# Seven products for three more units of the first block, column units set later, first weights in one run

## The chip, the core and the metric

The kernel runs on one core of a Trainium2 chip, in f32 throughout. The time is that of one launch, in device microseconds. Five engines run beside each other: TensorE (PE in the rows; its weight loads are PEld), VectorE (DVE), ScalarE (ACT), GpSimd (POOL) and SyncE (SP), which here only starts transfers. Matrix products land in eight banks of PSUM, called G[0] to G[3] and A[0] to A[3].

## The reference, cut to what matters

A sequence of 256 tokens of width 1024 goes through two blocks of two layers each. The first block, per layer:

```
h = rms_norm(x, pre_norm_g[l])
u = h @ w_in[l]                    # 352 + 768 + 768 + 512 + 1024 columns
u_mla, u_sb, u_moba, u_conv, u_gate = split(u)
o_a = mla_attention(...)           # low rank queries and keys, rotary part
o_b = stick_breaking_attention(qb, kb, vb)
o_c = moba_attention(qc, kc, vc, rel_bias)     # the third branch, 4 heads of 64
o_d = conformer_conv(u_conv, ...)  # 31 taps, layer norm, silu, product
y = concat([o_a, o_b, o_c, o_d]) * silu(u_gate)    # four gates of 256 columns
x = x + rms_norm(y @ w_out[l], post_norm_g[l])
```

With 256 tokens the third branch sees one block, so it is causal attention with a bias by distance. The second block is a gated linear attention layer and an attention layer, each followed by a network of width 4096 with a squared relu. Its shifts, scales and gates come from one row c through `w_ada`: `silu(c) @ w_ada[i] + b_ada[i]`.

## The kernel before

**Units.** All large weights come in units of 128 partitions x 2048 values (1 MB) through a ring of six slots, `raw`. SyncE loads unit n once unit n - 6 is released, strictly in order (L481 to L483). A layer of the first block has 30 units: 18 of weights, "w", and 12 column units, "a". A column unit holds columns of `w_ada`; VectorE multiplies it by the row silu(c) and sums along the row, in two halves (L983, `column_half`), for the second block. Two things set their place: the string `ORDER`, which is the order in the ring, and the calls `ada_unit(l, a)` in VectorE's program. I call them a0 to a11.

**The first block on TensorE.** In program order per layer: transposes of the normed tokens; the first weights (two units, `U_MLA0` and `U_MLA1`, each loaded in the first round as four runs of 352 values per partition); the convolution's two units; queries and keys of the second branch; the first branch's low rank products; the values (`U_V0`, `U_V1`); then `unit_t` for the third branch's queries and keys, `U_CQ` into G[0] and `U_CK` into G[1]; transposes of the first branch's queries and keys (L2182); suffix sums of the second branch (L2188 to L2192), which wait for `nl_ready`; and the loop over the four gates. Each turn g of that loop does the gate's unit in G[1] (L2005), the values of the pair before, two turns of transposed probabilities (L2032), and the scores of the next pair. Turn 0 also transposes the convolution's result (L2262), turn 2 transposes its normed form (L2269), which waits for `cnat_ready` of VectorE. A gate's unit waits for `silu_ready`, VectorE's product of the gate before out of G[1] (L1262). `unit_t` is 16 products of 128 x 128 by 256 columns, 32 records in the trace, since an f32 product is two records.

**VectorE in the same place.** Norms, rotary parts, the 31 taps of the convolution (L1030), the second branch's logarithms (L1237 to L1244, sums L1250), masks and row maxima of the scores (L1052, L1055), reciprocals (L1062), gates (L1262), the layer norm of the convolution (L1311 to L1321), and column units a0 to a10 between them. ScalarE does exponentials, tanh of gates, and copies out of PSUM.

**Seven products.** In the second block large products already run in Winograd's form: a 2 x 2 block product by seven products and sums, not eight products. `mixer_weights` (L1759 to L1764) builds four sums of a unit's blocks, `mixer_sums` (L1772 to L1782) adds up the seven results, `token_sums` (L1591 to L1595) builds the sums of the tokens.

**The network of the second block.** 15 groups of seven products; per group g VectorE does half sums, weight sums, rest sums, hidden sums, sums of a later unit, and from group 1 on a column unit of the second layer (`side_unit`). When the last one is done it computes two sets of coefficients (L1071 to L1085). Behind the last group come `seven_sums` (L1667 to L1684), the residual, and the boundary to the next stage.

## Time and profile before

| | |
|---|---|
| median of 3 runs | 970.14 us (969.9 to 970.84) |
| the profiled execution | 970.39 us, span 968.6 us |
| TensorE busy | 955.1 us, 99% of the span |
| VectorE busy | 759.3 us, 78% |
| ScalarE busy | 230.5 us, 24% |
| GpSimd busy | 83.2 us, 9% |
| transfers | 205.39 MB, 212 GB/s |
| granted clock of TensorE | 0.998 |

Times in the rows are microseconds from the start of the span. The first block's layer 0 lies between 7 and 156 us, its layer 1 between 156 and 301 us; from the second branch's values on they run alike, some 146.5 us apart. A busy share tells how full an engine is, not whether it is waited for: that is in the list of waits and in the idle time written in brackets behind a row of the timeline, with what ended it.

### The profile page before, as it was taken

The numbers are of one execution on the slowest core, as the hardware profiler recorded it, in microseconds if no ns is written. First come the engines' busy times: TensorE is split into PE (matmuls) and PEld (weight loads), VectorE is DVE, ScalarE is ACT, GpSimd is POOL, SyncE is SP. The second block draws the span as 40 slices with busy tenths as digits, with TensorE's granted clock in tenths as the row PEclk, the third lists the DMA queues.
The fourth block names the chain that finished last, engine by engine and source line by source line (L and its number), as shares of the span: only waits on it lengthen the run. The fifth ranks groups of instructions, "written<-read, shape, count | busy, mean of one in ns | idle before, by whom it ended". The sixth has DMA issues, their size and how long they took to land. (4 is left out here: it accounts for less than half of the span.)

```text
span 968.6 us, 14456 instructions
## 1 busy us (share of the span) xinstructions
PE 955.1 (99%) x5386; PEld 712.5 (74%) x5386; DVE 759.3 (78%) x1721; ACT 230.5 (24%) x580; POOL 83.2 (9%) x100
## 2 busy tenths in 40 slices
PE   8999999999999999999999999999999999999996
PEld 5858856858867998757777777689994777777764
DVE  2797687697688898999899988955667877766687
ACT  4134434125433222111000000123333200000002
POOL 2100000100001000000001000056830000000000
PEclk9999999999999999999999999999999999999999
DMA  9955553955555756473579677535443255544411
GB/s 347 365 211 210 213 222 133 369 198 231 193 225 208 294 218 256 177 300 132 218 294 357 259 306 261 196 131 196 153 175 137 100 199 174 217 174 174 174 44 44
DMA packets 31213, 205.39 MB, mean 212 GB/s; under 512 B 3655, under 2 KB 4860, under 8 KB 7852
## 3 DMA queue, kind: packets, MB, share of 16 engines
q1 hardware_dynamic: 27884, 190.94, 52.4%
q0 software_dynamic: 3264, 13.57, 3.7%
q8 instruction: 43, 0.70, 0.3%
q14 instruction: 22, 0.18, 0.1%
HBM read 203.42 MB, written 1.07 MB: 211 GB/s over the span
## 5 line engine op out<-in xcount | busy, mean ns | idle before, releaser
L2005 PE MATMUL bank<-hT,raw 128*128 128x256 f32 x704 | 155.6, 381 | 0.0
L2005 PEld LDWEIGHTS bank<-hT,raw 128*128 128x128 f32 x704 | 133.0, 190 | 19.8 <-issue 2.4
L983 DVE CUSTOM_DVE_ANT_0 raw<-raw,crow 128x1024 f32<-128x1024 f32 x96 | 114.1, 1232 | 9.2 <-DMA raw<-units_dram 7.7
L2364 PE MATMUL bank<-yT,arena 128*128 128x512 f32 x224 | 100.8, 593 | 0.5 <-DVE yT L1658 0.5
L2364 PE MATMUL bank<-raw,arena 128*128 128x512 f32 x180 | 86.9, 593 | 0.0
L2364 PEld LDWEIGHTS bank<-yT,arena 128*128 128x128 f32 x224 | 42.4, 190 | 53.3 <-issue 50.6
L2392 PEld LDWEIGHTS bank<-hT,raw 128*128 128x128 f32 x416 | 50.4, 192 | 11.5 <-issue 11.5
L841 ACT ACTIVATE arena<-bank 128x512 f32<-128x512 f32 x26 | 15.5, 598 | 177.6 <-PE bank L2392 177.6
L2392 PE MATMUL bank<-hT,raw 128*128 128x128 f32 x416 | 50.7, 275 | 0.0
L1030 DVE SCALAR_TENSOR_TENSOR arena<-arena 128x256 f32<-128x256 f32 x120 | 49.2, 486 | 0.1
L2364 PEld LDWEIGHTS bank<-raw,arena 128*128 128x128 f32 x180 | 30.1, 191 | 17.2 <-issue 17.2
L2392 PE MATMUL bank<-arena 128*128 128x128 f32 x336 | 42.2, 276 | 0.0
L2392 PE MATMUL bank<-arena,gateT 128*128 128x128 f32 x336 | 42.1, 275 | 0.0
L2392 PEld LDWEIGHTS bank<-arena 128*128 128x128 f32 x336 | 39.8, 192 | 1.2 <-issue 1.2
L2392 PEld LDWEIGHTS bank<-arena,gateT 128*128 128x128 f32 x336 | 39.8, 192 | 0.0
L2085 PE MATMUL bank<-arena 128*128 128x512 f32 x88 | 39.8, 592 | 0.0
L2392 PEld LDWEIGHTS bank<-arena,raw 128*128 128x128 f32 x224 | 29.4, 192 | 13.4 <-issue 13.4
L843 ACT ACTIVATE arena<-bank 128x384 f32<-128x384 f32 x28 | 13.7, 491 | 105.1 <-PE bank L2392 105.1
L2335 PE MATMUL bank<-hT,raw 128*128 128x128 f32 x244 | 37.4, 283 | 0.9 <-ACT hT L700 0.7
L1621 DVE TENSOR_TENSOR arena<-arena 128x256 f32<-128x256 f32 x26 | 11.0, 424 | 32.4 <-ACT arena L841 31.8
L2335 PEld LDWEIGHTS bank<-hT,raw 128*128 128x128 f32 x244 | 33.0, 191 | 3.8 <-issue 2.1
L2085 PEld LDWEIGHTS bank<-arena 128*128 128x128 f32 x88 | 16.6, 190 | 19.7 <-issue 19.6
(473 smaller groups left out, 1782.4 us busy)
## 6 DMA issues: line engine op xcount, KB each, us to landing
raw<-units_dram SPq DMA_DIRECT2D x178, 1024.0 KB, 4.9
arena<-ln_rows_dram POOLq DMA_DIRECT2D x4, 1024.0 KB, 5.9
arena<-gate_scratch POOLq DMA_DIRECT2D x4, 512.0 KB, 6.9
arena<-att_line_dram POOLq DMA_DIRECT2D x4, 512.0 KB, 5.2
arena<-small_dram POOLq DMA_DIRECT2D x2, 896.0 KB, 10.5
raw<-units_dram SPq DMA_DIRECT2D x2, 704.0 KB, 8.0
xt<-x_dram SPq DMA_DIRECT2D x2, 512.0 KB, 5.6
arena<-post_g_dram POOLq DMA_DIRECT2D x2, 512.0 KB, 8.5
```

The costliest lines, as they stand in the source:

```text
L841: act.activation(prod[:, 0:4].rearrange("p i n -> p (i n)"), A[0][:], ACT.Copy).then_inc(prod_ready.sem, 1)
L843: act.activation(prod[:, 4:7].rearrange("p i n -> p (i n)"), A[0][:, 0:3 * P], ACT.Copy).then_inc(prod_ready.sem, 1)
L983: ins = dve.tensor_tensor_reduce(out=w, in0=w, in1=crow[:], scale=1.0, scalar=0.0, op0=ALU.mult, op1=ALU.add, accum_out=dst[:, c:c + 1])
L1030: ins = dve.scalar_tensor_tensor(cacc[:, c, :], xg[:, c, j:j + S], w, cacc[:, c, :], ALU.mult, ALU.add)
L1621: ch.do(dve.tensor_tensor(csum[:, 0:5:4], p[:, 0:1].to_broadcast([P, 2, P]), p[:, 1:3], ALU.add))
L2005: mm = pe.matmul(b[:, c * S:(c + 1) * S], raw[:, s, k * 256 + c * P:k * 256 + (c + 1) * P], act_t[:, k, :], start=(k == 0), stop=(k == KC ...
L2085: mm = pe.matmul(OUT_BANKS[l][j][:], x[c] if isinstance(x, list) else x[:, c], y[c] if isinstance(y, list) else y[:, 512 * c:512 * (c + 1) ...
L2335: mm = pe.matmul(b[:, c * S + t * P:c * S + (t + 1) * P], raw[:, n % SLOTS, k * 256 + c * P:k * 256 + (c + 1) * P], hT[:, k, t * P:(t + 1) ...
L2364: mm = pe.matmul(SB[i][:], x, y, start=g == 0, stop=stop)
L2392: mm = pe.matmul(b[:, i * P:(i + 1) * P], x(k), y(k), start=k == 0, stop=k == 3)
```

## The change

1. Third branch's queries, its keys and the second gate go through seven products: 28 products of 128 x 128 by 128 columns a unit. New on VectorE are `first_tokens` (four additions a layer), `first_weights` (four additions and waits a unit) and `first_outputs` (six). ScalarE copies a unit's seven products out of PSUM in two parts. The keys go to A[2] and G[1], the second gate to G[1] and A[0]. Its tanh is taken from a buffer `early`, and the third gate's unit waits for ScalarE's copy of G[1] in place of VectorE's gate.
2. Column units: a3 (before in the middle of the taps) behind the logarithms; a4 and a5 (before behind the taps and the logarithms) behind the row maxima of the second pair of heads; a6 and a7 behind those of the third pair; a8 behind the normed convolution; a9 as before. `ORDER` is changed to match. In the first network column units go by halves, and from group 8 on they stand half a unit later.
3. The first two units are laid out without gaps, 1408 values in one run per partition.
4. Some small transfers share a semaphore; that is left out here.

```diff
-ORDER = "wwwawwawwawawawa" "wawawawa" "wwawwa"
+ORDER = "wwwawwawwa" "wwwa" "wwaaa" "waa" "wa" "wwawwa"
...
+U_SEVEN = (U_CQ, U_CK, U_G1)
...
-                w = [t.rearrange("p (k n) -> p k n", k=4)[:, :, 0:MLA_IN if s <= U_MLA1 else 512] for t in (raw[:, s, :], units[s, :, :])]
-                sp.dma_start(w[0], w[1]).then_inc(landed[s], 16)
+                c = slice(0, 4 * MLA_IN if s <= U_MLA1 else UNIT)
+                sp.dma_start(raw[:, s, c], units[s, :, c]).then_inc(landed[s], 16)
...
-                wait_used(act, T1 * l, U_CQ)
-                act.activation(qkC[:, 0], G[0][:], ACT.Copy, scale=HD_SCALE).then_inc(qk_ready.sem, 1)
-                wait_used(act, T1 * l, U_CK)
-                act.activation(qkC[:, 1], G[1][:], ACT.Copy).then_inc(qk_ready.sem, 1)
+                act.wait_ge(rope_ready.sem, rope_ready.at(l, 2))
+                for i, (u, b) in enumerate(((U_CQ, G[0]), (U_CK, A[2]))):
+                    scale = (HD_SCALE, 1.0)[i]
+                    act.wait_ge(fhalf_ready.sem, fhalf_ready.at(l, i + 1))
+                    act.activation(first_prod[i][:, 0:4].rearrange("p i n -> p (i n)"), b[:], ACT.Copy,
+                                   scale=scale).then_inc(fprod_ready.sem, 1)
...
+                def gate_copies(g):
+
+                    p = first_prod[(g + 1) % 2]
+                    act.wait_ge(qk_ready.sem, qk_ready.at(l, 2 + g))
+                    act.wait_ge(fhalf_ready.sem, fhalf_ready.at(l, g + 2))
+                    act.activation(p[:, 4:7].rearrange("p i n -> p (i n)"), A[0][:, 0:3 * P], ACT.Copy).then_inc(fprod_ready.sem, 1)
+                    wait_used(act, T1 * l, U_GATE[g])
+                    act.activation(p[:, 0:4].rearrange("p i n -> p (i n)"), G[1][:], ACT.Copy).then_inc(fprod_ready.sem, 1)
+
                 def gate_tanhs(g):
-                    wait_used(act, T1 * l, U_GATE[g])
+                    if g != 1:
+                        wait_used(act, T1 * l, U_GATE[g])
                     if g >= 1:
                         act.wait_ge(silu_ready.sem, silu_ready.at(l, g))
-                    act.activation(th[:].rearrange("p c s -> p (c s)"), G[1][:], ACT.Tanh, scale=0.5).then_inc(gate_tanh.sem, 1)
+                    if g == 1:
+                        act.wait_ge(qk_ready.sem, qk_ready.at(l, 5))
+                    act.activation(th[:].rearrange("p c s -> p (c s)"), gate_in if g == 1 else G[1][:], ACT.Tanh,
+                                   scale=0.5).then_inc(gate_tanh.sem, 1)
...
+            def first_tokens(l):
+
+                dve.wait_ge(ht_act.sem, ht_act.at(l, 12))
+                dve.wait_ge(ht_dve.sem, ht_dve.at(l, 4))
+                b = [[hT[:, 4 * k:4 * k + 4, t * P:(t + 1) * P] for t in range(NT)] for k in range(2)]
+                ch.do(dve.tensor_tensor(first_tsum[:, 0], b[0][1], b[0][0], ALU.subtract))
+                ch.do(dve.tensor_tensor(first_tsum[:, 2], b[1][1], b[0][1], ALU.subtract))
+                ch.sync(1)
+                ch.do(dve.tensor_tensor(first_tsum[:, 1], b[1][1], first_tsum[:, 0], ALU.subtract))
+                ch.sync()
+                dve.tensor_tensor(first_tsum[:, 3], b[1][0], first_tsum[:, 1], ALU.subtract).then_inc(fsum_ready.sem, 1)
+
+            def first_weights(l, i):
+
+                wait_landed(dve, T1 * l, U_SEVEN[i])
+                ch.pass_waits()
+                a, d = first_blocks(U_SEVEN[i]), first_sums[i]
+                ch.do(dve.tensor_tensor(d[1], a[0][0], a[1][0], ALU.subtract))
+                ch.sync()
+                ch.do(dve.tensor_tensor(a[1][0], a[1][0], a[1][1], ALU.add))
+                ch.sync()
+                ch.do(dve.tensor_tensor(d[0], a[1][0], a[0][0], ALU.subtract))
+                ch.sync()
+                dve.tensor_tensor(d[2], a[0][1], d[0], ALU.subtract).then_inc(fsum_ready.sem, 1)
+
+            def first_outputs(l, i, o):
+
+                p, c = first_prod[i % 2], first_tmp
+                dve.wait_ge(fprod_ready.sem, fprod_ready.at(l, 2 * i + 2))
+                ch.pass_waits()
+                ch.do(dve.tensor_tensor(c[:, 0], p[:, 0], p[:, 2], ALU.add))
+                ch.do(dve.tensor_tensor(o[:, 0], p[:, 0], p[:, 1], ALU.add))
+                ch.sync(1)
+                ch.do(dve.tensor_tensor(c[:, 1], c[:, 0], p[:, 3], ALU.add))
+                ch.do(dve.tensor_tensor(c[:, 2], c[:, 0], p[:, 5], ALU.add))
+                ch.sync(1)
+                ch.do(dve.tensor_tensor(o[:, 2:4], c[:, 1:2].to_broadcast([P, 2, P]), p[:, 4:6], ALU.add))
+                ch.sync(1)
+                ch.do(dve.tensor_tensor(o[:, 1], c[:, 2], p[:, 6], ALU.add))
+                ch.sync()
+                dve.sem_inc(qk_ready.sem, 1)
...
+                first_tokens(l)
...
-                taps(0, 12)
-                ada_unit(l, 3)
-                taps(12, 20)
+                taps(0, 20)
...
+                first_weights(l, 0)
+                first_weights(l, 1)
                 taps(20, TAPS)
-                ada_unit(l, 4)
...
-                ada_unit(l, 5)
-                ada_unit(l, 6)
+                ada_unit(l, 3)
+                for i in range(2):
+                    first_outputs(l, i, qkC[:, i].rearrange("p c (t n) -> p (c t) n", t=NT))
...
+                first_weights(l, 2)
                 for j in range(2 * H):
                     if j % 2 == 0:
-                        gate(j // 2)
+                        if j == 2:
+                            first_outputs(l, 2, early)
+                        else:
+                            gate(j // 2)
...
+                        if j == 2:
+                            gate(1)
                         if j < 6:
-                            ada_unit(l, 7 + j // 2)
+                            for a in ((4, 5), (6, 7), (9,))[j // 2]:
+                                ada_unit(l, a)
...
+                        ada_unit(l, 8)
...
-            def side_unit(lay, g, half=range(2)):
-
-                if lay == 0 and AG + g < len(ADA_1):
-                    ada_unit_1(ADA_1[AG + g], AG + g, half)
-                    if AG + g == len(ADA_1) - 1:
+            def side_half(lay, h):
+
+                n = AG + h // 2
+                if lay == 0 and n < len(ADA_1):
+                    ada_unit_1(ADA_1[n], n, (h % 2,))
+                    if n == len(ADA_1) - 1 and h % 2 == 1:
...
-                    if 0 < g < 8:
-                        side_unit(lay, g - 1)
-                    if g in (7, 8):
-                        side_unit(lay, 7, (g - 7,))
-                    if g >= 8:
-                        side_unit(lay, g)
+                    if g > 0:
+                        for h in range(2 * g - 2 + (g > 7), 2 * g + (g > 6)):
+                            side_half(lay, h)
...
+            def first_seven(l, i, b0, b1):
+
+                u = U_SEVEN[i]
+                a, d = first_blocks(u), first_sums[i]
+                h = [[hT[:, 4 * k:4 * k + 4, t * P:(t + 1) * P] for t in range(NT)] for k in range(2)]
+                x = [first_tsum[:, k] for k in range(4)]
+
+                def product(b, c, w, y):
+                    for k in range(4):
+                        mm = pe.matmul(b[:, c * P:(c + 1) * P], w[:, k], y[:, k], start=k == 0, stop=k == 3)
+                    return mm
+
+                def first_bank():
+                    product(b0, 0, a[0][0], h[0][0])
+                    product(b0, 1, a[0][1], h[1][0])
+                    pe.wait_ge(fsum_ready.sem, fsum_ready.at(l, i + 2))
+                    product(b0, 3, d[1], x[2])
+                    return product(b0, 2, d[0], x[1])
+
+                def second_bank():
+                    product(b1, 0, a[1][1], x[3])
+                    pe.wait_ge(fsum_ready.sem, fsum_ready.at(l, i + 2))
+                    product(b1, 2, d[2], h[1][1])
+                    return product(b1, 1, a[1][0], x[0])
+
+                wait_landed(pe, T1 * l, u)
+                pe.wait_ge(fsum_ready.sem, fsum_ready.at(l, 1))
+                if i < 2:
+                    first_bank().then_inc(fhalf_ready.sem, 1)
+                    if i == 1:
+                        pe.wait_ge(fprod_ready.sem, fprod_ready.at(l, 2))
+                    second_bank().then_inc(used[u % SLOTS], 1)
+                else:
+                    second_bank().then_inc(fhalf_ready.sem, 1)
+                    if i > 2:
+                        pe.wait_ge(fprod_ready.sem, fprod_ready.at(l, 2 * i))
+                    first_bank().then_inc(used[u % SLOTS], 1)
...
-                unit_t(T1 * l, U_CQ, hT, G[0])
-                unit_t(T1 * l, U_CK, hT, G[1])
+                first_seven(l, 0, G[0], G[1])
+                pe.wait_ge(upc_ready.sem, upc_ready.at(l, 6))
+                first_seven(l, 1, A[2], G[1])
...
-                    if g >= 1:
+                    if g == 0:
+                        pe.wait_ge(fprod_ready.sem, fprod_ready.at(l, 4))
+                    elif g == 2:
+                        pe.wait_ge(fprod_ready.sem, fprod_ready.at(l, 6))
+                    else:
                         pe.wait_ge(silu_ready.sem, silu_ready.at(l, g))
-                    unit_t(T1 * l, U_GATE[g], hT, G[1])
+                    if g == 1:
+                        pe.wait_ge(pt_ready.sem, 8 * l + 2 * g)
+                        first_seven(l, g + 1, G[1], A[0])
+                    else:
+                        unit_t(T1 * l, U_GATE[g], hT, G[1])
```


TensorE, where layer 0 comes to the third branch's queries and keys; before:

```order
L2015 MATMUL bank<-raw,hT 128x512 x16
L2161 MATMUL bank<-arena 128x256 x4
L2166 MATMUL bank<-arena 128x128 x4
L2005 MATMUL bank<-hT,raw 128x256 x32
L2182 MATMUL bank<-kst,arena 96x128 x16
```


and now:

```order
L2292 MATMUL bank<-arena 128x128 x4
L2173 MATMUL bank<-hT,raw 128x128 x8
L2173 MATMUL bank<-xs,gateT 128x128 x8
L2173 MATMUL bank<-xs,raw 128x128 x4
L2173 MATMUL bank<-hT,gateT 128x128 x4
L2173 MATMUL bank<-xs,raw 128x128 x4
L2173 MATMUL bank<-hT,raw 128x128 x8
L2173 MATMUL bank<-xs,yT 128x128 x8
L2173 MATMUL bank<-xs,raw 128x128 x4
L2173 MATMUL bank<-hT,yT 128x128 x4
L2173 MATMUL bank<-xs,raw 128x128 x4
L2310 MATMUL bank<-kst,arena 96x128 x16
```


The 32 products of 256 columns have become 56 of 128 columns. Those that read only `hT` and `raw` come first in the queries' unit; `gateT` and `yT` hold sums of the weights, `xs` those of the tokens.

VectorE in layer 0, between the row maxima of the second pair of scores and the third gate's product (`L1262`, now `L1344`); `ISA raw,acc<-raw,crow` is half a column unit; before:

```order
L1062 RECIPROCAL rinv<-rsum 128x2 x2
L983 ISA raw,acc<-raw,crow 128x1024
...
L1311 BN_STATS bst<-bank 128x6 x2
L1315 BN_AGGR bag<-bst 128x2 x2
L1317 TENSOR_SCALAR ms<-bag 128x2
L1262 SCALAR_TENSOR_TENSOR gateT<-arena,bank 128x512
...
L1062 RECIPROCAL rinv<-rsum 128x2 x2
L983 ISA raw,acc<-raw,crow 128x1024
...
L1321 TENSOR_SCALAR arena<-bank,bag,rs 128x256 x2
L1262 SCALAR_TENSOR_TENSOR gateT<-arena,bank 128x512
```


and now:

```order
L1143 RECIPROCAL rinv<-rsum 128x2 x2
L1022 ISA raw,acc<-raw,crow 128x1024
...
L1022 ISA raw,acc<-raw,crow 128x1024
...
L1400 BN_STATS bst<-bank 128x6 x2
...
L1106 TENSOR_TENSOR arena<-arena 128x128
...
L1143 RECIPROCAL rinv<-rsum 128x2 x2
L1344 SCALAR_TENSOR_TENSOR gateT<-arena,early 128x512
L1022 ISA raw,acc<-raw,crow 128x1024
...
L1022 ISA raw,acc<-raw,crow 128x1024
...
L1410 TENSOR_SCALAR arena<-bank,bag,rs 128x256 x2
L1022 ISA raw,acc<-raw,crow 128x1024
...
L1344 SCALAR_TENSOR_TENSOR gateT<-arena,bank 128x512
```


Where one column unit stood in front of the convolution's statistics (`BN_STATS`) there are two, the six additions of `first_outputs` (`L1106` and on) follow, the second gate's product stands behind the next maxima, then come two column units in place of one, and one more stands between the normed convolution and the third gate's product.

VectorE at the end of the first network, the last two groups (`gacc` column units, `L1071` to `L1085` the coefficients, `L1667` the first of the seven sums); before:

```order
L1614 TENSOR_TENSOR arena<-raw,arena 128x512
L983 ISA raw,gacc<-raw,crow 128x1024
...
L999 SCALAR_TENSOR_TENSOR gcol<-gacc,colb 128x8
L1071 TENSOR_TENSOR arena<-acc,colb 128x16
...
L1071 TENSOR_TENSOR arena<-acc,colb 128x16
...
L1621 TENSOR_TENSOR arena<-arena 128x2x128
...
L1653 TENSOR_TENSOR yT<-raw 128x512
...
L1658 TENSOR_TENSOR gateT<-gateT,raw 128x512
L1667 COPY arena<-bank 128x512
L1670 TENSOR_TENSOR arena<-arena,bank 128x512
```


and now:

```order
L1704 TENSOR_TENSOR arena<-raw,arena 128x512
L1022 ISA raw,gacc<-raw,crow 128x1024
...
L1711 TENSOR_TENSOR arena<-arena 128x2x128
...
L1743 TENSOR_TENSOR yT<-raw 128x512
...
L1748 TENSOR_TENSOR gateT<-gateT,raw 128x512
L1022 ISA raw,gacc<-raw,crow 128x1024
...
L1038 SCALAR_TENSOR_TENSOR gcol<-gacc,colb 128x8
L1152 TENSOR_TENSOR arena<-acc,colb 128x16
...
L1152 TENSOR_TENSOR arena<-acc,colb 128x16
...
L1757 COPY arena<-bank 128x512
L1760 TENSOR_TENSOR arena<-arena,bank 128x512
```


One half unit and both sets of coefficients have moved from ahead of group 13's rest to behind its last weight sums, directly in front of the seven sums.

## Rows read from the trace of the kernel before

**Rows 1.** The list of TensorE's waits: its line <- what ended the wait: us, times, longest.

```profile
PE bank L2058 <- DMA raw<-units_dram: 0.9, 2, 0.8
...
PE bank L2364 <- DVE yT L1658: 0.5, 1, 0.5
```

**Rows 2.** Busy time of VectorE by stretch: stretch, its length, busy us (instructions), clock, DMA share, GB/s.

```profile
43.48:119.01 75.53, 59.68 (x163) 1.00 0.57 214
191.07:265.48 74.41, 58.85 (x163) 1.00 0.56 212
```

**Rows 3.** VectorE's waits between 191.07 and 265.48 us.

```profile
DVE rinv L1062 <- ACT probs L637: 4.7, 5, 2.4
DVE gateT L1262 <- ACT arena L780: 4.6, 2, 2.9
DVE probs L1052 <- PE bank L2208: 2.6, 1, 2.6
DVE arena L1250 <- PE bank L2190: 2.0, 2, 1.4
```

**Rows 4.** TensorE in order of time: start, us, engine, line, out<-in, xcount [idle before].

```profile
42.83 7.07 PE L2005 MATMUL bank<-hT,raw 128*128 128x256 f32 x32
49.74 0.81 PE L2146 MATMUL bank<-arena 128*128 128x384 f32 x2
...
488.78 1.95 PE L2392 MATMUL bank<-hT,raw 128*128 128x128 f32 x16
...
492.35 1.88 PE L2364 MATMUL bank<-raw,arena 128*128 128x512 f32 x4
```

**Rows 5.** VectorE in order of time, second block's sums.

```profile
331.08 0.29 DVE L1774 TENSOR_TENSOR arena<-arena,bank 128x128 f32<-128x128 f32 x1
...
332.84 0.69 DVE L1759 TENSOR_TENSOR arena<-raw 128x512 f32<-128x512 f32 x1 [0.22 <-DVE arena L1782]
...
334.05 0.68 DVE L1762 TENSOR_TENSOR arena<-arena,raw 128x512 f32<-128x512 f32 x1
334.77 0.69 DVE L1764 TENSOR_TENSOR arena<-raw,arena 128x512 f32<-128x512 f32 x1
```

**Rows 6.** VectorE in order of time, the waits ahead of the column units.

```profile
31.49 0.75 DVE L1015 TENSOR_SCALAR arena<-arena 128x1024 f32<-128x1024 f32 x1 [3.28 <-ACT arena L727]
...
188.78 1.22 DVE L983 CUSTOM_DVE_ANT_0 raw<-raw,crow 128x1024 f32<-128x1024 f32 x1 [5.05 <-DMA raw<-units_dram]
```

**Rows 7.** VectorE's third gate product and TensorE's fourth gate unit, layer 1.

```profile
264.80 0.68 DVE L1262 SCALAR_TENSOR_TENSOR gateT<-arena,bank 128x512 f32<-128x512 f32 x1
...
266.41 7.17 PE L2005 MATMUL bank<-hT,raw 128*128 128x256 f32 x32
```

**Rows 8.** TensorE in order of time, the second unit of first weights.

```profile
12.10 2.63 PE L2058 MATMUL bank<-raw,hT 128*128 128x352 f32 x8 [0.77 <-DMA raw<-units_dram]
```

**Rows 9.** VectorE, then TensorE, at the end of the first network.

```profile
603.04 0.17 DVE L999 SCALAR_TENSOR_TENSOR gcol<-gacc,colb 128x8 f32<-128x8 f32 x1
...
605.14 0.43 DVE L1621 TENSOR_TENSOR arena<-arena 128x256 f32<-128x256 f32 x1 [0.50 <-DVE arena L1085]
...
615.78 0.69 DVE L1672 TENSOR_TENSOR arena<-arena,bank 128x512 f32<-128x512 f32 x1 [0.85 <-PE bank L2364]
616.70 0.69 DVE L1675 TENSOR_TENSOR arena<-arena,bank 128x512 f32<-128x512 f32 x1 [0.24 <-PE bank L2364]
...
619.54 0.69 DVE L1684 TENSOR_TENSOR arena<-arena,bank 128x512 f32<-128x512 f32 x1
...
625.53 0.69 DVE L1391 TENSOR_TENSOR arena<-bank,arena 128x512 f32<-128x512 f32 x1 [0.24 <-PE bank L2434]
...
632.28 1.04 PE L2102 MATMUL bank<-kst,xs 128*128 128x128 f32 x8
```

**Rows 10.** TensorE by stretch behind its last product: length, busy, clock, DMA share, GB/s.

```profile
962.00:964.00 2.00, 0.00 (x0) 1.00 0.53 201
964.00:966.00 2.00, 0.00 (x0) 0.52 0.11 39
```

More of the change, by code:

```diff
@@ L452, in build, with first_blocks @@
         out_block = [gateT[:].rearrange("p a b -> p (a b)")[:, 512 * i:512 * (i + 1)] for i in range(4)]
+        first_tsum = four(flat(xs))
+        first_sums = [[b[:, 512 * i:512 * (i + 1)].rearrange("p (k n) -> p k n", k=4) for i in range(3)]
+                      for b in (flat(gateT), flat(yT), nl, lbeta)]
+        first_sums.append([b.rearrange("p (k n) -> p k n", k=4) for b in (
+            flat(yT)[:, D:D + 512], flat(yT)[:, D + 512:2 * D], flat(cacc))])
+        first_prod = [b[:, 0:7 * P].rearrange("p (i n) -> p i n", i=7) for b in (mu_cn, flat4(qkB))]
+        first_tmp = rt[:].rearrange("p a b c d -> p (a b c d)")[:, 0:3 * P].rearrange("p (i n) -> p i n", i=3)
+        gate_in = early.rearrange("p i n -> p (i n)")
+        def first_blocks(u):
+            w = raw[:, u % SLOTS, :].rearrange("p (k n) -> p k n", k=KC)
+            return [[w[:, 4 * k:4 * k + 4, c * P:(c + 1) * P] for k in range(2)] for c in range(2)]
         def tile_banks(s, t):
@@ L2255, in _ @@
                     turn(8 * l, 2 * g, (A[3], A[0]))
+                    if g == 1:
+                        pe.wait_ge(fprod_ready.sem, fprod_ready.at(l, 2 * g + 3))
                     turn(8 * l, 2 * g + 1, (A[3], A[0]))
@@ L2839, in n_unit @@
 def n_unit(w, c0, half, width=512):
-    u = np.zeros((P, 4, 512), w.dtype)
-    u[:, :, :width] = w[half * 512:(half + 1) * 512, c0:c0 + width].reshape(4, P, width).transpose(1, 0, 2)
-    return u.reshape(P, UNIT)
+    u = np.zeros((P, UNIT), w.dtype)
+    u[:, :4 * width] = w[half * 512:(half + 1) * 512, c0:c0 + width].reshape(4, P, width).transpose(1, 0, 2).reshape(P, 4 * width)
+    return u
 def ada_gate(w, part, a):
```

62 lines of the change are left out of this document (36 added, 26 removed).

## The prediction

> **What bounds the kernel now.** I read the page's busy shares first, which the table above repeats: TensorE is busy 99% of the span. The list of TensorE's waits says what small part of the rest is to be had: two waits on the first weights, 0.9 us, and one on a weight sum of VectorE, 0.5 us [rows 1]. So in the two layers of the first block TensorE never waits, and the reader is to ask of each edit how much room the engine that feeds TensorE has left. That engine is VectorE: I took its busy time between two fixed points of each layer, from the end of column unit a2 (43.48 and 191.07 us) to the end of the third gate's product (119.01 and 265.48 us). It is busy 59.68 of 75.53 us and 58.85 of 74.41 us, so it idles 15.8 and 15.6 us [rows 2]. The list of its waits in layer 1 splits this idle time [rows 3]: 4.7 us on ScalarE's exponentials, 4.6 us on ScalarE's tanh of a gate, 2.6 and 2.0 us on TensorE's scores and suffix sums, and 1.7 us of small waits and gaps.
>
> **What the change gives TensorE.** A unit of 256 columns by plain products is 32 records in 49.74 - 42.83 = 6.91 us. By seven products of 128x128x512 it is 56 records. In the second block 32 such records take 492.35 - 488.78 = 3.57 us, 0.1116 us each [rows 4], so 56 take 6.25 us. Three units a layer and two layers save 6 x 0.66 = 4.0 us of TensorE's work. I cost this saving at nothing for the sum unless VectorE keeps up, which is the next step.
>
> **What it costs VectorE.** Per unit, the weight sums are four 128x512 additions, each waiting for the one before. The second block's sums show a dependent addition 0.72 us behind its predecessor (334.05, 334.77), and the last one takes 0.69 us with the next started some 0.05 us before its end, so a unit takes 3 x 0.72 + 0.64 = 2.8 us [rows 5]. The output sums are six additions, as the last six of the second block's, 332.84 - 331.08 = 1.76 us [rows 5]. Three units: 8.4 + 5.3 = 13.7 us a layer. The four token sums (2.6 us) go ahead of column unit a0 in layer 0, where VectorE waits 3.28 us for a tanh, and in layer 1 ahead of a1, where it later waits 5.05 us for a unit to land [rows 6]; both waits hide them, and without that cover they would add 2.6 us a layer. ScalarE's copies of products stand where copies of the same banks stood. The new wait of the third gate's unit for the copy of the second gate's products costs nothing: between the two units TensorE has the values of two branches, the transposes and the scores of a pair, while the copy needs 0.6 us; queued behind that wait is all of TensorE's work, so it would cost one for one if ScalarE came to it late.
>
> Column units a3 to a8 still stand between the two fixed points, all six, before and now: they are moved later, not out. Moving a3 and a4 behind lets the weight sums of the queries and keys go in early enough that TensorE doesn't wait there; but a4, a5, a6, a7 and a8 now all lie between the first gate's product and the third's, where two stood. So VectorE's stretch grows by 13.7 us and can shrink only by the waits that a later VectorE no longer meets. The tanh waits (4.6) go, since weight sums of the second gate and column units fill them; so do the waits on TensorE's scores and suffix sums (2.6 and 2.0), and I take half of the 1.7 that is left: 10.0 us. The 4.7 us on the exponentials stay, because each is a round trip that starts from VectorE's own row maximum. Bounds: if nothing of the 1.7 goes, 9.2; if all, 10.9.
>
> VectorE therefore ends the third gate's product 13.7 - 10.0 = 3.7 us later in layer 1. TensorE had 266.41 - 265.48 = 0.9 us of room between that product and the fourth gate's unit, which needs the same bank [rows 7]. So the fourth gate's unit starts 2.8 us late. In layer 0 the idle time is 0.3 us larger, so 2.5 us. The loss first shows at the four transposes of the normed convolution, L2269 before: they wait for VectorE, which reaches them one column unit too late, and the unit behind them waits again for the gate's product. I expect some 2.9 and 1.5 us of idle time on TensorE there, and a first, small wait of 0.3 to 0.6 us ahead of the second gate's unit. Behind the fourth gate VectorE catches up, since it had waits there; TensorE's delay stays as it is to the layer's end. TensorE's 2.0 us per layer are thus turned wholly into waiting.
>
> **The first weights.** The two first units come as 1408 contiguous values per partition in place of four runs of 352. TensorE waited 0.77 us for the second of them at 12.10 us [rows 8]. If the packets move faster this goes; the products of the first token tile then end by 13.8 us, and the second tile's input would have to be later than that to take the wait's place. All of layer 0 then starts earlier, VectorE's stretch too, since a2 is loaded when a0 is used, and a0 waits for a row that is loaded when the first units are used. I take -0.8 us; bounds 0 (same bytes, same rate) and -1.0.
>
> **The column units in the network.** From group 8 on a half unit is moved one group later, so the last half and the two coefficient sets fall behind the last weight sums, ahead of the sum of the seven products. Before, the set took 605.14 - 603.04 = 2.1 us, and it made the 0.5 us wait of [rows 1]; that goes. In its new place it is 1.15 + 0.1 + 2.1 = 3.3 us on VectorE in front of the seven sums. These had 0.85 + 0.24 us of waits on TensorE in them and gained 0.6 us by the lighter group before: 3.3 - 1.1 - 0.6 = 1.6 us late at 619.54 [rows 9]. Of this 0.24 us is absorbed at the residual (625.53), and TensorE's transposes at 632.28 had about 0.2 us of room, so they start 1.1 us late. I take +1.1 us in all; bounds -0.5 (the tail is hidden, the old wait gone) and +1.5.
>
> **Sum.** 2.5 + 2.8 - 0.8 + 1.1 = 5.6 us. The profiled run took 970.39 us for a span of 968.6, and the median is 970.14, so execution and median agree: 970.14 + 5.6 = 975.7 us. The remaining edits (shared semaphores, a moved wait for a small load) touch nothing that waits.
>
> **The rivals.**
> First, faster: TensorE stays the bound. It would need the 4.7 us of exponential waits to be filled as well, or the sums to be cheaper than in the second block; then a layer gains its 2.0 us, the start 0.8 and the network 0.5: 970.14 - 5.3 = 964.8. For it: TensorE is busy 99% and VectorE idles 15 us a layer. Against it: 13.7 us of new work against 10 us of idle time that can be used, and all column units in the same stretch.
> Second, no difference: VectorE's loss is 1.5 to 2 us a layer smaller than I count, because an output sum or a column unit slips into a round trip of the exponentials, and the network's tail is hidden. 5.6 - 4 - 1 gives about 970.7.
> Third, slower by another way: TensorE's clock. It was granted 1.00 in 962 to 964 us, two microseconds and more after the last product, and 0.52 in 964 to 966 [rows 10]; so an idle stretch of somewhat under four microseconds leaves the clock whole. I expect 2.9 us, a short burst and 1.5 us. If these together count as idle, the fourth gate's unit of 7.1 us [rows 7] runs at 1.2 in place of 2.4 GHz and takes as much again, 2 x 7 us more: 989. The point from which it decides is an idle stretch about one microsecond longer than I expect. The Trainium skill ("TensorE: Matmul & The Clock Gate", section "HAM oscillation — how this bites in real kernels") says that a matmul kernel's idle gaps past a certain length bring the engine back to half clock; by that rule the trace agrees, since only the gap at the end shows it and the short gaps do not.
> That the change doesn't do what it says, as a fourth: the pace of [rows 4] needs weight loads hidden behind 128-column products; here the stationary side is as in the second block, so I give it nothing of its own.
>
> **How the numbers follow.** My forecast 0.74, its own range 972.5 to 978; first rival 0.12; second 0.10; third 0.04. About 1.9 us (0.2%) is what a measurement can tell from no change. Faster 0.12, same 0.14 (the second rival and the low edge of the forecast), slower 0.74. The range of 8 in 10 leaves out the first rival and the clock: 970.8 to 978.3.
>
> **What would show it.** Right: on TensorE two waits of a few us in each layer, on VectorE's normed convolution and on its third gate's product, with VectorE without a wait other than on the exponentials between the a2 unit and that product; seven-product units at 6.25 us; no wait on the second first-weights unit; a wait ahead of the second tile boundary after the first network. Wrong: TensorE without waits in both layers (first rival), VectorE's sums under 2.5 or 1.5 us a unit, or a granted clock under 0.9 near 120 and 265 us.

## The result: 1.2% slower, and the profile after

| | before | after |
|---|---|---|
| median of 4 runs | 970.18 us (969.9 to 970.84) | 981.88 us (980.95 to 982.56) |
| ratio to before | | 1.0117 (95%: 1.0105 to 1.0129) |
| profiled execution, span | 968.6 us | 979.2 us |
| granted clock of TensorE | 0.998 | 0.991 |
| VectorE busy | 759.3 us | 786.7 us |

The forecast was 975.7 us, range 970.8 to 978.3: the direction was right, the time lies 3.6 us outside the range. The list of TensorE's waits, against [rows 1]:

```profile
PE bank L2407 <- DVE arena L1410: 5.1, 2, 2.5
PE bank L2093 <- DVE gateT L1344: 1.6, 2, 1.4
PE bank L2126 <- POOL eps_x L511: 1.3, 1, 1.3
PE bank L2228 <- DVE xs L1517: 0.9, 2, 0.8
...
PE bank L2564 <- DVE arena L1774: 0.5, 1, 0.5
```

The two waits that were forecast are there: 2.5 us at the transposes of the normed convolution (L2407) in each layer, and the fourth gate's unit (L2093) on the third gate's product. All waits together have grown from 4.5 to 11.7 us, 7.2 us, and the seven products take 4.0 us off TensorE. That makes 3.2 us, but the span is 10.6 us longer. So the waits are not the larger part, and a reader must look at what TensorE does behind them. TensorE in order of time, layer 0, then layer 1:

```profile
115.80 0.88 PE L2120 MATMUL bank<-kst,probs 128*128 128x128 f32 x6
119.22 1.12 PE L2407 MATMUL bank<-kst,arena 128*128 128x128 f32 x4 [2.54 <-DVE arena L1410]
...
122.11 8.79 PE L2093 MATMUL bank<-hT,raw 128*128 128x256 f32 x32 [0.18 <-DVE gateT L1344]
...
270.79 0.66 PE L2407 MATMUL bank<-kst,arena 128*128 128x128 f32 x4 [2.55 <-DVE arena L1410]
...
273.67 9.79 PE L2093 MATMUL bank<-hT,raw 128*128 128x256 f32 x32 [1.37 <-DVE gateT L1344]
```

The fourth gate's unit, 32 records as before, takes 8.79 and 9.79 us where it took 7.17 [rows 7]. TensorE by stretch (length, busy, granted clock, DMA share, GB/s) says why:

```profile
116.60:118.40 1.80, 0.08 (x1) 1.00 1.02 423
118.40:125.60 7.20, 6.19 (x21) 0.53 0.99 389
125.60:127.60 2.00, 2.00 (x11) 1.00 0.29 119
268.20:270.80 2.60, 0.05 (x2) 1.00 1.01 422
270.80:272.00 1.20, 1.20 (x12) 1.00 0.98 416
272.00:279.20 7.20, 5.83 (x17) 0.53 0.77 307
279.20:281.20 2.00, 2.00 (x11) 1.00 0.00 0
```

TensorE ran at 1.2 in place of 2.4 GHz for some 7 us in or behind each stall. In layer 0 the clock fell while the engine was idle; in layer 1 the idle time had ended, 1.2 us of work were done at full clock, and then it fell. On the page the clock's line of 40 digits shows one 8 and the mean only 0.991: a loss of this size is not seen there.

The steps, read as the delay of one and the same product of TensorE against the trace of before: the start 0.0 us; layer 0 up to the fourth gate's unit 2.2 us, up to the convolution's product behind it 3.8; layer 1, counted from its own start, 3.6 and 6.2 at the same two places; the first network 0.9; sum 10.8, of which 0.2 are given back in the first rows of the second block.

The other rows that answer: the seven-product units (two from 69.35 to 81.96 us, one from 97.79 to 104.13) take 6.3 us each, [rows 4] gave 6.25. The weight sums take 2.78 us a unit (213.33 to 216.11), the output sums 1.70 (235.37 to 237.07), [rows 5] gave 2.8 and 1.76.

### The profile page after: what moved, and what is told of

Same layout as the page of the kernel before. It is cut to its first block and busy times, and to the rows that moved or that the text cites. A ratio compares the mean times of both kernels' runs of the same rounds, so it can differ in the third digit from the quotient of the medians.

```text
span 979.2 us, 14852 instructions
## 1 busy us (share of the span) xinstructions
PE 958.3 (98%) x5530; PEld 716.9 (73%) x5530; DVE 786.7 (80%) x1789; ACT 234.3 (24%) x588; POOL 84.2 (9%) x100
## 5 line engine op out<-in xcount | busy, mean ns | idle before, releaser
L2093 PE MATMUL bank<-hT,raw 128*128 128x256 f32 x512 | 117.5, 390 | 1.6 <-DVE gateT L1344 1.6
L2093 PEld LDWEIGHTS bank<-hT,raw 128*128 128x128 f32 x512 | 99.4, 196 | 18.2 <-DVE gateT L1344 2.7
L2530 PEld LDWEIGHTS bank<-hT,raw 128*128 128x128 f32 x416 | 50.4, 192 | 11.5 <-issue 11.5
L882 ACT ACTIVATE arena<-bank 128x384 f32<-128x384 f32 x28 | 13.7, 491 | 105.1 <-PE bank L2530 105.1
L2473 PEld LDWEIGHTS bank<-hT,raw 128*128 128x128 f32 x244 | 33.0, 191 | 3.5 <-issue 2.1
```

The costliest lines, as they stand in the source:

```text
L882: act.activation(prod[:, 4:7].rearrange("p i n -> p (i n)"), A[0][:, 0:3 * P], ACT.Copy).then_inc(prod_ready.sem, 1)
L2093: mm = pe.matmul(b[:, c * S:(c + 1) * S], raw[:, s, k * 256 + c * P:k * 256 + (c + 1) * P], act_t[:, k, :], start=(k == 0), stop=(k == KC ...
L2473: mm = pe.matmul(b[:, c * S + t * P:c * S + (t + 1) * P], raw[:, n % SLOTS, k * 256 + c * P:k * 256 + (c + 1) * P], hT[:, k, t * P:(t + 1) ...
L2530: mm = pe.matmul(b[:, i * P:(i + 1) * P], x(k), y(k), start=k == 0, stop=k == 3)
```

## The experiments

Each was timed beside the kernel before (970.3 to 970.5 us in these runs).

**Stalls made on purpose in the kernel before.** GpSimd fills a dead tile two, four or seven times, and TensorE waits for it once a layer, where the changed kernel stalls. VectorE isn't late in these kernels.

```diff
+ pool.wait_ge(ptp_ready.sem, 8 * l + 6)
+ for i in range(4):                       # 2, 4 or 7
+     pool.wait_ge(idle_done, 4 * l + i)   # 4 stands for the number of fills
+     pool.memset(zeros[:], 0.0).then_inc(idle_done, 1)
...
  pe.wait_ge(cnat_ready.sem, cnat_ready.at(l, 2))
+ pe.wait_ge(idle_done, 4 * (l + 1))
```

> The kernel before with two fills of a dead tile on GpSimd, about 0.5 us each, that TensorE waits for ahead of the four transposes of the normed convolution, once a layer; nothing else changed. TensorE should idle about 1.2 us there, twice. Theory 1 (an idle stretch of about 2.5 us on TensorE lowers its clock for a while, and this is where the difference between forecast and result lies): 1.2 us is too short, the granted clock stays at 1.00, and the time is that of before plus 2.4 us, 972.6. Theory 2 (stalls cost their own length and no more; the difference lies in VectorE's work): the same 972.6.

> The same with four fills: TensorE idles about 2.4 us twice, in a kernel in which VectorE is not late. Theory 1: the granted clock falls to about 0.5 for 6 to 7 us behind each, as in the changed kernel, and each stall costs 2.4 us and some 3 us more: 970.2 + 10.8 = 981. Theory 2: 970.2 + 4.8 = 975.0 with the clock at 1.00 or with dips that cost nothing.

> The same with seven fills: TensorE idles about 4.2 us twice. Theory 1: the clock falls and comes back some 6.5 us after the work goes on; the surcharge on the stall is again about 3 us, not more, so 970.2 + 2 x 7.2 = 984.6. Theory 2: 970.2 + 8.4 = 978.6.

Measured: 973.05 us (1.0033, 1.0021 to 1.0045), 978.79 (1.0095, 1.0080 to 1.0111) and 984.35 (1.0142, 1.0127 to 1.0158). The stalls are 1.38, 2.54 and 4.29 us long. With four fills the two layers differ, though their stalls are equal; TensorE in order of time:

```profile
120.90 0.63 PE L2279 MATMUL bank<-kst,arena 128*128 128x128 f32 x4 [2.54 <-POOL zeros L553]
...
122.32 7.17 PE L2014 MATMUL bank<-hT,raw 128*128 128x256 f32 x32
...
270.10 1.08 PE L2279 MATMUL bank<-kst,arena 128*128 128x128 f32 x4 [2.54 <-POOL zeros L553]
...
272.70 7.56 PE L2014 MATMUL bank<-hT,raw 128*128 128x256 f32 x32
```

and by stretch, four fills first, then seven:

```profile
120.90:128.00 7.10, 7.10 (x38) 1.00 0.37 152
...
270.00:273.60 3.60, 3.50 (x14) 0.53 0.77 323
273.60:280.00 6.40, 6.40 (x31) 1.00 0.00 0
```

```profile
121.60:128.60 7.00, 5.88 (x20) 0.51 0.29 122
```

So one and the same stall of 2.54 us cost next to nothing beyond itself in layer 0, and 1.6 us more in layer 1, where the clock was at half for 3.6 us. Over the four runs of this kernel the times are 977.02, 978.75, 978.84 and 980.51 us: steps of about 1.7 us, with the mean clock going from 0.995 to 0.992. Behind 4.3 us the clock is at half for 7.0 us in both layers, and each stall costs 7.2 us of delay, 2.9 more than its length. Behind 1.4 us it stays whole, and a stall costs 1.6 us. Two fills don't part the theories (both had 972.6). With seven, theory 1 (the clock) holds, 984.35 against its 984.6. With four the time lies between the theories (981 and 975.0): at 2.5 us it is not certain whether and for how long the clock falls.

**The same work on VectorE, TensorE kept busy.** Eleven products on data that nobody uses, ahead of TensorE's wait for the convolution in the changed kernel:

```diff
+ pe.wait_ge(nm_ready.sem, 8 * l + 6)
+ for _ in range(11):
+     pe.matmul(A[1][:, 0:S], ident, hT[:, 0, :], start=True, stop=True)
  pe.wait_ge(cnat_ready.sem, cnat_ready.at(l, 2))
```

> The changed kernel with eleven idle-filling products (128x128x256, into a bank that the next scores overwrite, their results unused) on TensorE ahead of its wait for the normed convolution, 2.4 us by 0.22 us each, in the place of most of the 2.5 us wait; VectorE's work is as it was. Theory 1: the granted clock stays at 1.00 through both layers, the fourth gate's unit takes 7.1 us in place of 8.8 and 9.8, and the time falls by 5 to 6 us to about 976.3. Theory 2: the stall is VectorE's and stays whatever fills it; 981.9 within 0.5.

Measured: 976.55 us (1.0065, 1.0052 to 1.0079), 5.3 us under the changed kernel. I had counted a product as one record of 0.22 us; it is two, so the eleven took 4.9 us and not 2.4:

```profile
116.22 4.91 PE L2406 MATMUL bank<-hT,kst 128*128 128x256 f32 x22
120.97 0.60 PE L2410 MATMUL bank<-kst,arena 128*128 128x128 f32 x4
...
122.35 7.17 PE L2093 MATMUL bank<-hT,raw 128*128 128x256 f32 x32
```

The filler thus pushed the transposes 1.8 us further back than the stall had, yet the fourth gate's unit starts at 122.35 (122.11 with the stall), since that waits for VectorE anyhow, and it takes 7.17 us. The granted clock is 1.00 through both layers. What the clock had cost is 4.2 us in the two traces (delay behind layer 1, from the start of layer 0: 9.9 against 5.7 us) and 5.3 between the medians.

**What makes VectorE late.** First the second gate's unit back to plain products, which takes 4.6 us of sums a layer off VectorE:

```diff
- U_SEVEN = (U_CQ, U_CK, U_G1)
+ U_SEVEN = (U_CQ, U_CK)
```

(and its sums, copies and waits as in the kernel before).

> The changed kernel with the second gate's unit as 32 plain products of 256 columns; queries and keys stay by seven products, column units stay where the change put them. VectorE has 4.6 us a layer less, TensorE 0.66 us more. Theory 1 (VectorE's lateness makes the stalls, 2.7 and 4.5 us of waits, and these make the clock fall, 2 x 3.4 us): both go, a layer gains 1.3 us on before, and with 0.7 us lost in the network the time is 970.2 - 2.6 + 0.7 = 968.3, the granted clock at 1.00 near 120 and 270 us. Theory 2 (the moved column units make the stall whatever the gate's product does, since they stand ahead of the normed convolution): waits of 1 to 2.5 us stay, 972 to 976.

Measured: 979.79 us (1.0097, 1.0082 to 1.0113). Theory 1, my own, fails: the stalls stay (2.0 us at the transposes in each layer, 1.3 us behind them in layer 0) and so do 7 us of half clock in each. Theory 2 has the stalls right, but its 972 to 976 is missed too, by 3.8 us; it had no term for the clock. The waits of VectorE on a gate's tanh (2.7 us) and on the scores (2.05 us) are back, which the sums had filled. Next the converse, the change's places for the column units alone, put into the kernel before with no sum of seven products in it:

```diff
- ORDER = "wwwawwawwawawawa" "wawawawa" "wwawwa"
+ ORDER = "wwwawwawwa" "wwwa" "wwaaa" "waa" "wa" "wwawwa"
...
- ada_unit(l, 7 + j // 2)
+ for a in ((4, 5), (6, 7), (9,))[j // 2]:
+     ada_unit(l, a)
```

(a3 behind the logarithms, a8 behind the convolution's scaling, as in the change).

> The kernel before with the change's places for the first block's column units (and their order of loading) and nothing else: all units by plain products. Theory 1, the forecast's (VectorE's new sums, 13.7 us a layer, outgrow the waits of the stretch): without them VectorE has 15 us a layer to spare, no stall, 970.2 within 1. Theory 2, from the run without the second gate's seven products (the waits of VectorE are bound to single places, and the second column unit between the last pair's scores and the normed convolution, with the one behind it, makes the stall by itself): TensorE idles about 2.0 us at the transposes and 1.3 us or less ahead of the fourth gate's unit in each layer, and the clock falls there: 970.2 + 4 to 6.5 + 3.4 to 6.8, 978 to 983.

Measured: 982.69 us (1.0128, 1.0112 to 1.0143), as slow as the change itself. VectorE in order of time, the kernel before, from the last pair's scores on:

```profile
110.22 0.29 DVE L1052 CUSTOM_DVE_ANT_0 probs<-bank,arena 128x128 f32<-128x128 f32 x1 [2.62 <-PE bank L2208]
...
112.96 1.23 DVE L983 CUSTOM_DVE_ANT_0 raw<-raw,crow 128x1024 f32<-128x1024 f32 x1
...
115.25 0.17 DVE L966 TENSOR_SCALAR guess<-ms 128x2 int32<-128x2 int32 x1
...
117.42 0.99 DVE L1321 TENSOR_SCALAR arena<-bank,bag,rs 128x256 f32<-128x256 f32 x2
```

and with the column units moved:

```profile
110.27 0.29 DVE L1052 CUSTOM_DVE_ANT_0 probs<-bank,arena 128x128 f32<-128x128 f32 x1 [2.05 <-PE bank L2206]
...
113.01 1.23 DVE L983 CUSTOM_DVE_ANT_0 raw<-raw,crow 128x1024 f32<-128x1024 f32 x1
...
117.60 0.17 DVE L966 TENSOR_SCALAR guess<-ms 128x2 int32<-128x2 int32 x1
...
119.77 1.00 DVE L1318 TENSOR_SCALAR arena<-bank,bag,rs 128x256 f32<-128x256 f32 x2
```

In both, VectorE stands idle for two microseconds and more until TensorE gives it the third pair's scores. Nothing that it did before that idle time matters: the count starts anew at 110.2 us, when TensorE delivers. From there the convolution was ready at 118.41 us, 0.15 us ahead of TensorE's transposes at 118.56. A second column unit in this place, 2.3 us, is late by 2.1 us whatever VectorE has to spare elsewhere: in this kernel it is busy 59.92 of the 80.15 us from 43.50 to 123.65, and 20 us of idle time didn't help. Theory 2 holds.

The changed kernel itself shows the same. VectorE in order of time:

```profile
108.18 0.29 DVE L1133 CUSTOM_DVE_ANT_0 probs<-bank,arena 128x128 f32<-128x128 f32 x1 [0.60 <-DVEq L130]
...
110.83 0.67 DVE L1344 SCALAR_TENSOR_TENSOR gateT<-arena,early 128x512 f32<-128x512 f32 x1
...
118.17 1.00 DVE L1410 TENSOR_SCALAR arena<-bank,bag,rs 128x256 f32<-128x256 f32 x2
...
121.37 0.68 DVE L1344 SCALAR_TENSOR_TENSOR gateT<-arena,bank 128x512 f32<-128x512 f32 x1
```

With all its sums done it still idles 0.60 us ahead of the third pair's scores. From there to the end of the third gate's product it takes 13.87 us, where it took 8.79 (110.22 to 119.01): two column units more (4.6 us) and the second gate's product, which the change put behind these scores (0.6). The scores come 2.0 us earlier, since TensorE has saved that much by then. That makes the third gate's product 3.0 us late (122.05 against 119.01), by places alone.

**All three units by seven products, VectorE's steps in another order.** First the convolution's root and scaling ahead of a6 and a7, and a8 behind the third gate's product:

```diff
- for a in ((4, 5), (6, 7), (9,))[j // 2]:
+ if j == 2:
+     inv_root(2 * l + 2, 2)
+     ...                                # cnat, moved here from j == 3
+ for a in ((4, 5), (6, 7), (8, 9))[j // 2]:
```

> The changed kernel, all three units by seven products, with two steps of VectorE moved: the normed convolution's root and scaling ahead of column units a6 and a7, and a8 behind the third gate's product. VectorE's sum of work is the same. Theory 1: the wait at the transposes goes, one wait of 1.7 to 2 us ahead of the fourth gate's unit stays in each layer, too short for the clock to fall; it eats the 2.0 us that a layer's seven products save, so 970.2 + 0.7 + 0.3 = 971.2. Theory 2 (any stall of VectorE of 1.7 us or more brings the clock down): 971.2 + 3.4 to 6.8 = 975 to 978.

Measured: 973.53 us (1.0037, 1.0024 to 1.0051). The transposes don't wait, the fourth gate's unit waits 1.84 us in each layer, and the clock stays whole, as theory 1 has it. The time is 2.3 us above it: layer 1 doesn't come out even but loses 1.9 us, with 0.7 us of small waits (0.3, 0.2 and 0.2) that layer 0 hasn't, and the network takes 1.1. Then the column units spread over the single waits:

```diff
+ ada_unit(l, 4)
  head_inverse(8 * l, 0)
...
- for a in ((4, 5), (6, 7), (9,))[j // 2]:
+ for a in ((5, 6), (7,), (8, 9))[j // 2]:
```

> The changed kernel, all three units by seven products, with column units at other places on VectorE: a4 between the first two heads' row maxima and their reciprocals (where VectorE waits 2.7 us for the exponentials), a5 and a6 behind the second pair's scores, a7 alone behind the third's, a8 behind the third gate's product. VectorE's sum of work is the same. Theory 1 (sum of work): with the 2.3 us of a4 now in the wait for the exponentials and a8 moved out, VectorE still has all other work, 4 us of the stalls go and the sum comes to before's time within 1.5. Theory 2 (places): TensorE waits under 0.5 us a layer in the stretch, both layers gain their 2.0 us, and with 1 us lost in the network the time is 970.2 - 4.0 + 1.0 = 967.2.

Measured: 969.29 us (0.9988, 0.9978 to 0.9997), 0.1% faster than before, 12.6 us under the change with the same instructions. A whole column unit fits into the wait for the exponentials; VectorE in order of time:

```profile
90.42 1.22 DVE L1022 CUSTOM_DVE_ANT_0 raw<-raw,crow 128x1024 f32<-128x1024 f32 x1
91.56 0.08 DVE L1022 DVE_READ_ACCUMULATOR2_ANT acc<- 128x1 f32 x1
91.56 1.22 DVE L1022 CUSTOM_DVE_ANT_0 raw<-raw,crow 128x1024 f32<-128x1024 f32 x1
92.71 0.08 DVE L1022 DVE_READ_ACCUMULATOR2_ANT acc<- 128x1 f32 x1
93.25 0.17 DVE L1143 RECIPROCAL rinv<-rsum 128x2 f32<-128x2 f32 x1 [0.46 <-ACT probs L653]
```

TensorE waits 0.3 us at the transposes in each layer. It gains 1.3 us in layer 0, but only 0.3 in layer 1, and theory 2's time is missed by 2.1 us for that. Last, the seven products with the column units where the kernel before has them:

```diff
- ORDER = "wwwawwawwa" "wwwa" "wwaaa" "waa" "wa" "wwawwa"
+ ORDER = "wwwawwawwawawawa" "wawawawa" "wwawwa"
...
+ ada_unit(l, 3)                         # in the taps; a4 behind them, a5 and a6 behind the logarithms
...
- for a in ((4, 5), (6, 7), (9,))[j // 2]:
+ for a in ((7,), (8,), (9,))[j // 2]:
```

> The changed kernel, all three units by seven products, with the first block's column units where the kernel before has them (and loaded in its order). Theory 1 (only the move of the column units costs anything; the new sums fit in VectorE's waits wherever they stand): the layers' 4.0 us are gained whole, less 1.0 for the network: 967.2. Theory 2 (places count for the new sums too): VectorE is without a wait from 197 us to the logarithms' masked products at 232.8 in the changed kernel, which TensorE takes up at once, and 2.4 us early in layer 0; a3 and a4 ahead of them, 4.6 us, make TensorE wait some 4.4 and 2.2 us there, a6 ahead of the first rows' maxima about 1 us more ahead of the first heads' transposes, and the clock falls at least in layer 1: 970.2 - 4.0 + 1.0 + 8.9 + 3.4 = 979.5, 977 to 983.

Measured: 982.1 us (1.0122, 1.0105 to 1.0139). It is over theory 2's 979.5 but inside its 977 to 983. TensorE in order of time, layer 1:

```profile
238.07 1.48 PE L2313 MATMUL bank<-kst,arena 128*96 128x128 f32 x8 [4.63 <-DVE arena L1328]
...
253.20 1.19 PE L2123 MATMUL bank<-kst,probs 128*128 128x128 f32 x6 [0.71 <-ACT probs L660]
```

The clock is at half for 3.6 us behind this wait and behind that of 2.96 us in layer 0. So the column units did have to move for the sums of seven products; it is where they went that costs.

**The first weights, and the network.**

```diff
- w = [t.rearrange("p (k n) -> p k n", k=4)[:, :, 0:MLA_IN if s <= U_MLA1 else 512] for t in (raw[:, s, :], units[s, :, :])]
- sp.dma_start(w[0], w[1]).then_inc(landed[s], 16)
+ c = slice(0, 4 * MLA_IN if s <= U_MLA1 else UNIT)
+ sp.dma_start(raw[:, s, c], units[s, :, c]).then_inc(landed[s], 16)
```

(and the matching offsets on TensorE and in the layout of the weights in memory).

> The kernel before with nothing changed but the two first weight units, 1408 contiguous values a partition in place of four runs of 352. Theory 1 (the forecast's term): the wait of 0.8 us for the second unit goes, 969.4. Theory 2 (the bytes and not the runs set the landing, as the changed kernel's trace says, where the second unit's products start at 12.07 us in place of 12.10): 970.2 within 0.3.

Measured: 970.27 us (0.9996, 0.9987 to 1.0005). The time is theory 2's, but the interval reaches from 1.3 us less to 0.5 more, so theory 1's 969.4 isn't excluded. In the changed kernel's trace the second unit's products start at 12.07 in place of 12.10 us [rows 8], with a wait of 0.52 us on the transfer and 0.3 us on ScalarE ahead of the first. Single executions scatter more than this: these products start at 11.55 to 12.15 us in the traces of the five kernels with four runs and at 11.18 to 12.28 us in the nine with one. Whether the layout is worth 0 or 0.8 us stays open.

Then the halves of the network's column units in their old groups, first in the changed kernel, then in the kernel with the column units spread (969.29 us), which the second expectation calls the last kernel:

```diff
- for h in range(2 * g - 2 + (g > 7), 2 * g + (g > 6)):
+ for h in range(2 * g - 2 + (g > 7) + (g > 8), 2 * g + (g > 6) + (g > 7)):
```

> The changed kernel with the halves of the network's column units in the old groups, so that the two coefficient sets stand ahead of the last weight sums again. Theory 1 (the new place costs, as forecast; in the trace the network gives TensorE 0.75 us more delay): TensorE's 0.5 us wait at the products of group 13 is back, the two on the seven sums and on the second block's first rows go, 981.9 - 0.8 = 981.1. Theory 2 (the new place is hidden): 981.9 + 0.5.

> The last kernel with the network's halves in their old groups too. If the new groups cost what the two traces of that edit say (0.4 us in the profiles, 1.8 between the medians), 966.5 within 0.7; if the difference of those medians came from the start and the clock, the same as the last kernel within 0.5.

Measured: 980.12 us (1.0101, 1.0086 to 1.0117) in the changed kernel, 1.8 us less than with the new groups, below both theories; the intervals of the two ratios overlap. The two traces are 0.9 us apart. They show 0.4 us in the network and 0.9 at the start, which is the scatter just named, while the layers go 0.6 the other way. The waits on the seven sums and on the second block's first rows go; the 0.5 us wait at group 13 is not back. In its place TensorE idles 0.64 us at 525.40 us for no reason that the profile shows; without that the network's difference would be 1.0. With the column units spread it is 967.77 us (0.9973, 0.9963 to 0.9984), 1.5 us less, and the two traces show 1.4 of it in the network. Neither reading of that expectation is met: the time is 0.6 us over the first's range and outside the second's. The new groups do cost, between 0.4 and 1.5 us. This last kernel beats both the kernel before, by 2.5 us, and the changed one, by 14.1.

## Why the prediction was wrong

The mechanism was right in its outline: the seven-product units took the time that was forecast and so did their sums, TensorE's 4.0 us turned into waits on VectorE at the two places named, the first in each layer at the normed convolution. The direction followed. Its own sign of being wrong came too: the granted clock was 0.53 from 118.40 and from 272.00 us. Two steps don't stand, the clock and the reason for VectorE's lateness; the start and the network follow with their sizes.

**The clock, the step that puts the time outside the range.** "So an idle stretch of somewhat under four microseconds leaves the clock whole" was read from one row behind the last product [rows 10]. One instance showed that a gap can be that long, and I took it for a bound. Stalls of 2.54 us brought the clock down in both layers of the changed kernel, and those of 2.04 us did so in the run with the second gate by plain products. The page of the Trainium skill that the prediction named ("TensorE: Matmul & The Clock Gate", section "HAM oscillation — how this bites in real kernels") says that gaps past a certain length do this in a matmul kernel; the runs here agree in kind, but gaps shorter than the page names, from 2.04 us on, were enough. The price was wrong too, and in the other direction: the rival's 2 x 7 us supposed a whole unit at half clock in addition (975.7 + 14.2 is 989.9, where the text has 989); the unit lost 1.6 and 2.6 us, and the filler run puts the whole at 4.2 to 5.3 us. With the clock kept whole by the filler the time is 976.55 us, 0.8 over the forecast of 975.7. A chance of 0.04 and a price of 14 us stood where near certainty and 4 to 5 us belonged. In layer 0 the half clock ahead of the fourth gate's unit cost nothing (a delay of 2.2 us there, 2.4 us in the filler run at full clock), because TensorE waited there for VectorE in any case.

**VectorE's stretch, right in size by luck.** The sum took all of VectorE's new work, 13.7 us, against 10.0 us of idle time of the whole stretch, 3.7 us too much. Measured without the clock's part, the two layers lose 5.7 us where the forecast had 2.5 + 2.8. But in the run with the column units moved and no new sum TensorE stalls nearly as long (2.05 us at the transposes, 1.37 more in layer 1), and with 4.6 us of sums taken away again the stalls stay. Idle time cannot be added up over a stretch: each wait for TensorE starts VectorE afresh, and only the work between the last such wait and the instruction that TensorE needs counts. Counted so, the third gate's product is 3.0 us late in layer 0, where the forecast had 3.4 (2.5 and the 0.9 of room). The rows for it were in the trace of before: the scores at 110.2, the scaling's end at 118.41, the transposes at 118.56 us, 0.15 us of room against 2.3 us of a second column unit. The words "they are moved later, not out" named the cause and the sum then passed over it. That the exponentials' 4.7 us stay held for the changed kernel (4.8 us in layer 0), but not because each is a round trip: with a column unit of 2.3 us put into the first of these waits, in the kernel with the column units spread, they come to 2.9 us.

In layer 1 the delay was 3.6 in place of 2.8 us. There column unit a2 landed late: VectorE waited 5.98 us for it, and it starts 1.5 us later against TensorE than before. In the filler run it is 0.5 us late by the same measure, the 0.9 us that TensorE loses ahead of the second gate's unit in the changed kernel isn't lost, and the layer's delay is 3.1 us. That the late unit is the cause is thus likely, not shown; which earlier transfer holds it up I have not tried.

**The start, -0.8 us, was 0 in the trace,** the lower end of the bounds. The layout alone gave a median 0.1 us lower, with an interval that holds both 0 and -0.8, so this term isn't settled.

**The network, +1.1 us, was 0.9** (1.1 and 1.3 in the traces of two other kernels), by the way that was given: the sum of the seven products ends 1.4 us late, and the second tile's first rows wait 0.8 us for it.

Put together: 5.7 + 0.0 + 0.9 gives 6.6 us, against a forecast of 5.6; the clock adds 4.2 in the trace, 10.8. Neither other rival came: TensorE didn't stay the bound. A gain can be had, though: a version with the same products runs in 967.8.

## What to carry to other kernels

To cost work that is moved on an engine with idle time, find for each instruction that another engine waits for the last wait ahead of it, and add up what stands between the two; idle time further back can't pay for it. A stall of TensorE of two microseconds and more cost up to 2.9 us more in clock here, so shorter ones, or products of no use in the gap, can be cheaper than one long one. And put movable work into the waits of round trips between engines, such as the one from row maxima over exponentials to reciprocals.

## What the runs showed of the hardware

- After a stall of 1.38 us or of 1.84 us the granted clock stayed at 1.00 (four instances of two kernels). After stalls of 2.04 to 4.63 us it fell in 13 of 14 instances (the changed kernel, six of the experiments); the one exception is a stall of 2.54 us. It was at half in a stretch of 3.6 or of 7.0 to 7.2 us (mean 0.51 to 0.53 of each), and not longer behind the longer stalls: 3.6 us behind 4.63 us, 7.2 us behind 2.04 us.
- The fall can come when the stall is over: in layer 1 of the changed kernel after 1.2 us of work at full clock.
- A stall delays what follows by about 0.2 us more than it shows: 1.38 us by 1.57, 2.54 us at full clock by 2.73, since a product's record otherwise overlaps the one before: in the kernel before, the transposes start at 118.56 us, 0.17 us ahead of the end of the row before them (117.85 + 0.88).
- A float32 product leaves two records in the trace: eleven products of 256 columns were 22 records, 0.22 us apart.
